# Order of the two token halves between the linears: sums of both halves ahead of both normed rows

## What is computed

```python
def rmsnorm(x, g):
    y = x * lax.rsqrt(jnp.mean(x * x, axis=-1, keepdims=True) + RMS_EPS)
    return y * g

x = x + FFN_RESIDUAL * rmsnorm(swiglu(rmsnorm(x, g[0]), w_in, w_out), g[1])   # first block
h = rmsnorm(x, g[2])                                                          # what the next linear reads
gate = jax.nn.sigmoid(rmsnorm(x, g[6]) @ ple_w_gate[i])
x = x + rmsnorm(gate * (p[i] @ ple_w_proj[i]), g[7])
h = h + 0.5 * swiglu_2(rms_norm(h, norm_ffn1), w_ffn1_in, w_ffn1_out)         # second block: no norm of y
```

## Time and profile before

| | us |
|---|---|
| median of 3 runs | 1823.16 |
| lowest, highest | 1822.29, 1826.94 |
| profiled execution, device time | 1826.12 |
| its span in the trace | 1824.3 |
| PE busy in the span | 1734.6 |
| DVE, ACT, POOL busy | 1090.7, 881.3, 166.6 |

### The profile page before, as it was taken

One profiled execution on the slowest core, in us unless ns is written; L12 is line 12 of the kernel. 1 busy time (PEld: TensorE's weight loads), 2 busy tenths in 40 slices (PEclk: granted clock), 3 DMA queues, 4 the chain that ended last, 5 costly groups with the idle time before them and its releaser, 6 DMA issues.

```text
span 1824.3 us, 28207 instructions
## 1 busy us (share of the span) xinstructions
PE 1734.6 (95%) x11999; PEld 1588.3 (87%) x11999; DVE 1090.7 (60%) x1410; ACT 881.3 (48%) x1370; POOL 166.6 (9%) x192
## 2 busy tenths in 40 slices
PE   7999999999998999999999998999999997999996
PEld 6899799899977998989789997899989887899994
DVE  5455567678766544658565555655566575655554
ACT  5344466544564455453454445544454444444443
POOL 0000001218001002800000000000000000000000
PEclk9999999999999999999999999999999998999998
DMA  6655433454544544531445554465544331455551
GB/s 226 237 188 187 178 139 139 160 190 179 199 158 153 182 170 143 185 116 47 184 155 176 187 199 146 163 221 184 185 159 177 122 111 70 158 206 185 185 185 69
DMA packets 51086, 300.99 MB, mean 165 GB/s; under 512 B 6073, under 2 KB 12689, under 8 KB 17169
## 3 DMA queue, kind: packets, MB, share of 16 engines
q1 hardware_dynamic: 50800, 298.66, 45.7%
q0 software_dynamic: 160, 0.52, 0.1%
HBM read 298.08 MB, written 1.09 MB: 164 GB/s over the span
## 4 chain that ended last, share of the span: by engine, by line
PE 75%; ACT 9%; DVE 7%; DMA 3%; issue 2%; POOL 1%; SPq 1%; DVEq 0%; ACTq 0%; POOLq 0%
PE PS L1799 72%; DVE wlo L1109 3%; ACT whi L634 3%; DMA raw<-in_w 2%; PE PS L1802 2%; ACT wk L677 2%; POOL st L526 1%; DVE xn L1194 1%; ACT SC L766 1%; PE PS L1919 1%; DVE X L1186 1%; ACT SC L854 1%; DMA SC<-in_pT 0%; POOL st L519 0%; PE PS L2099 0%
## 5 line engine op out<-in xcount | busy, mean ns | idle before, releaser
L1109 DVE TENSOR_TENSOR wlo<-raw,whi 128x1024 fp32r<-128x1024 f32 x528 | 661.3, 1262 | 445.3 <-ACT whi L634 444.5
L634 ACT ACTIVATE whi<-raw 128x1024 fp32r<-128x1024 f32 x528 | 549.7, 1053 | 412.6 <-PE PS L1799 254.3
L1799 PE MATMUL PS<-xhi,whi 128*128 128x256 f32 x2536 | 724.9, 286 | 5.8 <-DVE wlo L1109 5.2
L1799 PE MATMUL PS<-xhi,wlo 128*128 128x256 f32 x2536 | 719.3, 284 | 0.0
L1799 PE MATMUL PS<-xlo,whi 128*128 128x256 f32 x2536 | 710.3, 283 | 0.0
L1799 PEld LDWEIGHTS PS<-xhi,whi 128*128 128x128 f32 x2536 | 489.6, 193 | 14.1 <-DVE wlo L1109 7.0
L1799 PEld LDWEIGHTS PS<-xhi,wlo 128*128 128x128 f32 x2536 | 489.7, 193 | 0.0
L1799 PEld LDWEIGHTS PS<-xlo,whi 128*128 128x128 f32 x2536 | 484.2, 192 | 2.0
L1799 PE MATMUL PS<-whi,hhi 128*128 128x512 f32 x544 | 170.2, 394 | 2.5 <-DVE wlo L1109 2.5
L1799 PE MATMUL PS<-wlo,hhi 128*128 128x512 f32 x544 | 168.5, 391 | 0.0
L1799 PE MATMUL PS<-whi,hlo 128*128 128x512 f32 x544 | 168.3, 390 | 0.0
(11 more groups left out here) (261 smaller groups left out, 1454.7 us busy)
## 6 DMA issues: line engine op xcount, KB each, us to landing
raw<-in_w SPq DMA_DIRECT2D x264, 1024.0 KB, 4.8
gr<-in_rows SPq DMA_DIRECT2D x23, 512.0 KB, 3.8
SC<-scratch SPq DMA_DIRECT2D x1, 2048.0 KB, 12.1
SC<-scratch SPq DMA_DIRECT2D x2, 1024.0 KB, 11.7
X<-in_x SPq DMA_DIRECT2D x2, 512.0 KB, 4.9
xn<-in_sc SPq DMA_DIRECT2D x2, 512.0 KB, 6.8
out<-xn SPq DMA_DIRECT2D x2, 512.0 KB, 2.7
SC<-in_pT SPq DMA_DIRECT2D x3, 256.0 KB, 4.1
```

Of the source, the lines that this page charges most:

```text
L634: a.activation(whi[:, u % NSPLIT, :], raw[:, u // 2 % NRAW, u % 2 * HU:u % 2 * HU + HU], ACT.Copy).then_inc(s_hi, 1)
L1109: v.tensor_tensor(wlo[:, u % NSPLIT, :], src, hi.bitcast(f32), SUB).then_inc(s_lo, 1)
L1799: return pe.matmul(o, l, r, start=start, stop=stop)
```

## The change

Every list of steps gets a seventh step, and the tuples are new. In the new order each engine does the sums of squares of y, the product with g1 and the residual sum of both halves, and only then the norm, transposes and evictions of both halves. On DVE the first step of a half is now the gate's product (gated stages) or the product with g1 of the high columns; the low columns, or the whole product with g1 in a gated stage, come as the second step. Four tuples serve the kinds of stage. For `DEFER` stages the new tuple gives the same sequence as before on every engine. On ACT the gated stages do the sigmoid of half 1 ahead of the squares of half 0. The count of the semaphore `s_sq` follows the new order. PE's fillers: half 0 now also waits for half 1's sum and issues four more behind it, and half 1 has four fillers and no waits for events. Nothing that is computed changes.

```diff
-ORDER = (0, 0, 0, 1, 0, 1, 1, 0, 1, 0, 1, 1)
-ORDER_PLACED = (0, 0, 0, 1, 0, 1, 1, 0, 1, 0, 1, 1)
-ORDER_DEFER = (0, 0, 0, 1, 0, 1, 0, 1, 0, 1)
+BOTH = (0, 1, 0, 1, 0, 1, 0, 1)
+ORDER = (0, 0, 1, 0, 1, 1) + BOTH
+ORDER_GATED = (0, 0, 1, 1, 0, 1) + BOTH
+ORDER_LAST = (0, 0, 0, 1, 1, 1) + BOTH
+ORDER_DEFER = (0, 0, 0, 0, 1, 1, 0, 1, 0, 1, 0, 1)
...
-n_sq = counts([n + 2 for n in N_SQ1])
+n_sq_first = counts([n + 2 for n in N_SQ1])
+def n_sq(k, h, i=None):
+    n = N_SQ1[k]
+    if k in DEFER:
+        return n_sq_first(k, h, i)
+    i = n + 1 if i is None else i
+    return n_sq_first(k, 0, 0) + (h * n + i if i < n else n + 2 * h + i)
...
-            for i, h in enumerate(ORDER_DEFER if k in DEFER else ORDER_PLACED if k == PLACED else ORDER):
+            for i, h in enumerate(ORDER_DEFER if k in DEFER else ORDER_LAST if k == STORED else ORDER_GATED if k in GATED else ORDER):
...
-                take_turns(k, (none, post_r, norm_r, none, none, none))
+                take_turns(k, (none, none, post_r, norm_r, none, none, none))
...
-            steps = (squares, none, squares2, none, evict_hi, none)
+            steps = (none, squares, none, squares2, none, evict_hi, none)
...
-                settle(k, {3: project})
+                settle(k, {5: project})
...
-            def times_g(k, h):
+            def gate_or_high(k, h):
                 if k in GATED:
                     gated(k, h)
+                elif k in POST:
+                    y, g1 = y_of(k, h), row_in(ROW_G1[k])
+                    y_ready(q, k, h)
+                    if k == PLACED:
+                        q.wait_ge(s_cst, 16)
+                    v.tensor_tensor(xn[:, h, HI], y[:, HI], g1[:, HI], MUL).then_inc(s_yg, 1)
+
+            def times_g(k, h):
                 if k not in POST:
                     return
                 y, g1 = y_of(k, h), row_in(ROW_G1[k])
                 if k in GATED:
                     q.wait_ge(s_gated, 2 * GATED.index(k) + h + 1)
                     v.tensor_tensor(xn[:, h, :], y, g1, MUL).then_inc(s_yg, 1)
-                    return
...
+                else:
+                    q.wait_ge(s_sq, n_sq(k, h, 0))
+                    v.tensor_tensor(xn[:, h, LO], y[:, LO], g1[:, LO], MUL).then_inc(s_yg, 1)
...
-            steps = (times_g, add_x, none, norm, place_u, evict_lo)
+            steps = (gate_or_high, times_g, add_x, none, norm, place_u, evict_lo)
...
                 b = tr_bank(k, h, 0)
+                if h and k not in DEFER:
+                    fill_in(b, LAST[BEFORE[k]] + 1, 4)
+                    return
...
                 turn_idle(b, s_X, n_x(k, h, 1))
+                if k not in DEFER:
+                    turn_idle(b, s_X, n_x(k, 1, 1))
...
-            steps = (none, none, none, none, transposed, none)
+            steps = (none, none, none, none, none, transposed, none)
```

More of the change, by code:

```diff
@@ L1251, in rest @@
                     evict_lo(k, 1)
-                take_turns(k, steps, {3: lambda: linear(f"proj{layer}", 2, head=2, tail=0)})
+                take_turns(k, steps, {5: lambda: linear(f"proj{layer}", 2, head=2, tail=0)})
                 linear(f"gate{layer}", 8, head=4, tail=2, finish=rest)
```

## The result

The changed kernel takes 1807.17 us (median of 4 runs, 1802.59 to 1809.24); the kernel before, on the same chip with one more run, 1824.42 us. The ratio is 0.9901 with a 95% interval of 0.9876 to 0.9927: faster by 17.3 us. The profiled execution took 1809.24 us with a span of 1807.4, against 1826.12 and 1824.3 before: 16.9 us less. Forecast were 1806.5 and a range of 1801 to 1813. In all the runs that follow, one single execution, of the experiment with the gates not in front, took 3389.2 us and is left out of its median.

A forecast was written before the change was run, and what follows sets the result against it. Half 1's sum, queued on DVE behind half 0's normed row, was taken to bound the stages. Eight stage gains sum to 16.7 us: 1823.16 - 16.7 = 1806.5 us, range 1801 to 1813.

The forecast's parts named there:

- What bounds a stage: Between linears, half 1's sum on DVE waits behind half 0's normed row; what that sum wins, the stage wins.
- Rival E: Whole kernel: PE's 95% busy share is real work, so nothing can be won; 1823 us, chance 0.02.
- Rival C: In eight stages half 0's later work sets the end, each 0.8 us longer; 1829.5 us, chance 0.03.
- Stages 2, 4, 6, 8: Half 1's sum and transposes come earlier; gains taken as 2.1, 4.15, 1.8 and 2.6 us.
- Stages 9 and 10: Half 1's sum comes 2.0 us earlier, four extra fillers cost 0.3 on the path; gain 1.67 us each.
- Stage 12: Half 1's sum 2.54 us earlier, less 0 to 0.5 for a root beside half 0's row; gain 2.3 us.
- Stage 5: ACT's 20 copies, starting with half 0's transposes, set the end; gain taken as 0.4 us (-0.5 to 0.8).
- The clock: PE's 1.2 GHz stretches behind stages 9 and 10 go as its waits shrink; 2.8 us in all.
- Rival A: POOL's roots between linears cost 1.2 us per meeting with DVE; 9.1 us back, 1815.6 us, chance 0.12.
- Rival B: At the linears, weight transfers don't keep up; half the gain returns as waits for `wlo`; 1815 us, chance 0.08.

The follow-up runs named there:

- gates not in front: Changed kernel with half 0's sum again ahead of half 1's gate and g1 product (stages 2, 4, 5, 6, 8), both sums still before both rows; 1816.5 us.
- with PE free: Changed kernel with half 1's sum behind half 0's normed row on DVE and eight PE fillers moved behind half 0's transposes; 1825.24 us.
- without late fillers: Changed kernel without the four fillers behind half 1's sum and the four between the two halves' transposes; 1810.88 us.
- The first experiment: Changed kernel with only DVE's list changed: half 1's residual sum behind half 0's normed row again; 1835.87 us.
- stage 5 old: Changed kernel with stage 5 alone in the order of before on all engines; 1807.97 us.
- eight fillers: Changed kernel with eight fillers in place of four behind each of the two sums in stage 5 alone; 1806.93 us.
- roots on DVE: Changed kernel with POOL's roots between the linears replaced by a sum and plain reciprocal on DVE, so another output; 1802.43 us.
- old order with few fillers: Kernel before with only PE's fillers of half 1 changed: four behind half 1's sum, none behind its earlier events; 1823.39 us.

## Why the prediction was right

**What bounds a stage** held: half 1's sum behind half 0's row. Put back, with PE free, it loses 18 us. Rival E (nothing can be won) falls with the result itself. Rival C (half 0 decides, and each stage gets longer) falls as well, since seven of eight stages got shorter and the eighth did in the second profile, but its mechanism is there at a small size: in stages 2, 4, 6 and 8 half 1's transposes stand 1.03 us behind their row, for 0.81 in the run without late fillers, so half 0's transposes and the fillers in PE's queue decide by 0.2 us. The first experiment produced the same thing by force, at 10 us.

**Stages 2, 4, 6, 8.** The terms were right in kind, and each gain came out 0.1 to 0.3 short. For the most part POOL was stretched more than I charged: half 0's row starts 3.66 us behind its sum in the gated stages, for the 3.39 that I took. In stage 6, 0.1 of the 0.3 is that I took 1.8 where the sum gave 1.68. In stage 4 half 1's sum stands 6.79 us behind the gate's product (573.84 + 1.33 - 568.38) for 9.18 before. I had its gain at 2.47, it was 2.39. Transposes behind the sum: 5.22 for the 5.1 of the sum.

**Stages 9 and 10** gave 1.9, not 1.67: the step that put four fillers on the path was wrong, by 0.2 us. Half 1's transposes start 0.80 behind its row (1347.45 in the timeline, 1348.25), so its own chain set the end, not PE's queue.

**Stage 12** gave 1.86 for 2.3. The sum came 2.54 earlier, to the hundredth. Then it took 3.99 us to half 1's row (1798.94 to 1802.93) for 3.31 before: 0.68 for half 1's last root, whose two instructions took 0.68 and 0.83 us beside half 0's row for 0.29 and 0.55 before, above the 0 to 0.5 I had charged.

**Stage 5** is the step that failed in the first profile, -0.97 for 0.4. What failed is the size: the copies started 11.35 us behind y, beyond even the low end. The run again, at 10.18, shows that a stretch at half clock made most of it, a thing that the prediction names for eight transposes in rival C (1.97 for 1.03) but gives no place in stage 5's working. Half 0's row, which I put at 0.7 to 1.2 us later than before, came 1.56 later in the first profile and 1.27 in the second. Undisturbed, the gain is 0.2, inside the range given for it.

**The clock.** 2.8 us forecast, 2.7 found, in stages 9 and 10. That the new order is what earns it is shown only in part. In six profiles of kernels with the new sums and the late fillers (after, stage 5 old, eight fillers, gates not in front, roots on DVE, the changed kernel again) no stretch at half clock falls behind 9 or 10, twelve times in twelve. In the new order without late fillers both got one, in the kernel before both, in the first experiment stage 9, in the old order with few fillers and with PE free neither. That speaks for the new sums and late fillers together holding the clock there, but the kernel without late fillers has one profile only, and two kernels of another order kept the clock as well; the cause stays open. The Trainium skill ("TensorE: Matmul & The Clock Gate", Part 1) says that the point at which the clock rises shifts from run to run. The trace agrees and goes further: in stage 5 one program had a stretch in one profile (0.62) and none in the next (1.00).

**Luck.** That the forecast of 1806.5 fell within 0.7 us of the 1807.17 is partly luck. It was the median before less the stages' 16.7, with nothing for the clock. The stages gave 14.5, 2.2 less, and the clock 2.7, and the two cancel. Against the profiled run's own time I had 19.5 us, and 16.9 came.

**Rival A, the port,** is there, at a smaller size. It wanted 1.6 us less gain in each of stages 2, 4, 6 and 8 and 0.9 in 9, 10 and 12; the gains came out short by 0.1 to 0.3 in the first four, by nothing in 9 and 10 and by 0.4 in 12. The sign that I had named, a power of 0.8 to 0.9 us and not 1.4 where it meets DVE, came only in part. POOL's power takes 1.51 or 1.52 us beside a product with two inputs in SBUF, once in each of stages 4, 6 and 8 (there the product reads `SC`, in SBUF, where the prediction had counted on products that read PSUM), and 0.83 to 0.87 beside the sums and rows that began before it, and POOL is busy 8.3 us more. But the 1.52 lies under DVE's work on half 1, which goes on till 573.33, so that only 0.51 of it shows. In stages 9 and 10 the sum reads y from PSUM, and POOL's power beside it takes what it takes alone:

```profile
1344.04 0.56 POOL L539 TENSOR_TENSOR st<-st 128x1 f32<-128x1 f32 x1
```

(the sum ran from 1344.01 to 1345.30). The Trainium skill ("SBUF — State Buffer", Who interferes with whom) says that a DVE instruction with two SBUF inputs contends with a GpSimd one that reads SBUF, and that one with at most one SBUF input, outside the 2-port modes, doesn't. The trace agrees: 0.55 or 0.56 with one such input, 0.83 to 1.52 with two, where DVE's instruction began first.

**Rival B, weights,** didn't come: 17.2 us of stage gains against 16.9 of span leave 0.3 that the linears can have given back, and PE waited 14.3 us in all for `wlo`, for 13.3 before.

## What to carry to other kernels

Where two halves share an in-order engine and only the later one's end counts, put the later half's first link ahead of the earlier half's last one; count what is behind it from there, hop by hop. Fillers that are to keep the clock up belong behind events that are early, and have to be few enough to be done when the real work comes. Undo each part of a change by itself; two parts can each be worth half of the gain or more, since one makes the other pay. A single profile can lay a stretch at half clock on any stage: run the same program again before explaining one microsecond.

## What the runs showed of the hardware that I had not expected

Where PE's stretches at half clock fell decided 0.9 us in one stage of one and the same program, and what stands in PE's queue ahead of a late event cost 10.6 us between two kernels that differ only in the place of eight fillers a stage (1835.87 and 1825.24). With the roots on DVE, its small instructions of one column took 0.16 to 0.21 us each, and a dependent pair 0.44 up to its user. Over POOL the pair and the way to its user took 0.96 where POOL met nothing, but there DVE is free meanwhile: half 1's row in stage 4 gained only 0.5 us.
